# A twenty-first expert weight unit, and an output projection that gives its weights back unit by unit, in a two-layer decoder trunk

## The reference

```
for i in range(2):
    mod = cond @ ada_w[i] + ada_b[i]                 # six vectors of 1024
    h = modulate(rms_norm(x, norm_mix[i]), sh_m, sc_m)
    y = diff_attention(h, ...) if i == 0 else mla_attention(h, ...)   # each ends in "@ w_o"
    x = x + g_m * y
    h = modulate(rms_norm(x, norm_ffn[i]), sh_f, sc_f)
    x = x + g_f * hier_moe(h, ...)   # 4 groups x 8 experts, top-1 group, top-2 experts in it
```

## Time and profile before

| | |
|---|---|
| median of 3 runs | 1125.56 us (1124.77 to 1127.2) |
| the profiled execution: its own time | 1125.21 us |
| the profiled execution: span of the trace | 1123.4 us |
| busy in the span: PE / DVE / ACT / POOL | 93% / 54% / 29% / 8% |
| moved by DMA | 341.44 MB, mean 304 GB/s |
| share of the chain that ended last: PE / DMA / DVE | 72% / 10% / 8% |

### The profile page before, as it was taken

How to read it: one execution, slowest core, us unless ns; L and a number is a source line. 1 busy time by engine, 2 the same in 40 slices (tenths; PEclk the granted TensorE clock), 3 DMA queues, 4 the chain that set the end, 5 groups by cost and what they waited for, 6 DMA issues and landing times.

```text
span 1123.4 us, 15296 instructions
## 1 busy us (share of the span) xinstructions
PE 1041.6 (93%) x5662; PEld 633.0 (56%) x5662; DVE 610.0 (54%) x1467; ACT 326.9 (29%) x889; POOL 92.1 (8%) x129
## 2 busy tenths in 40 slices
PE   7999999999998999897889999999998899979986
PEld 5444444656467666564556566555457666646652
DVE  6899989898647322222246577877236622222224
ACT  4321112874231111111114555665122211111110
POOL 1000000000011112121000000000001112101100
PEclk8999999999998999999999999999998999999999
DMA  9929868928569999999996400502717899999998
GB/s 367 405 89 378 354 259 322 419 101 325 200 255 372 408 419 420 417 418 419 419 386 275 164 1 1 188 1 84 329 75 277 351 420 420 418 413 419 420 415 336
DMA packets 66814, 341.44 MB, mean 304 GB/s; under 512 B 11110, under 2 KB 11366, under 8 KB 36400
## 3 DMA queue, kind: packets, MB, share of 16 engines
q1 hardware_dynamic: 49952, 297.68, 65.5%
q0 software_dynamic: 15120, 37.63, 8.6%
q10 hardware_dynamic: 1664, 5.09, 1.2%
HBM read 320.90 MB, written 37.24 MB: 319 GB/s over the span
## 4 chain that ended last, share of the span: by engine, by line
PE 72%; DMA 10%; DVE 8%; ACT 4%; issue 3%; SPq 3%; DVEq 0%; ACTq 0%; POOLq 0%
PE PP L956 17%; PE PP L722 10%; PE PP L832 10%; PE PP L971 8%; DMA ring<-in_moe_w 3%; DMA ring<-in_ada_t 3%; PE PP L744 3%; PE PP L1173 3%; PE PP L1139 2%; PE PP L1177 2%; PE PP L929 2%; PE PP L792 2%; SPq L566 2%; DMA X<-kept_d 2%; PE PP L781 2%
## 5 line engine op out<-in xcount | busy, mean ns | idle before, releaser
L722 PE MATMUL PP<-ring,AHS 128*128 128x512 f32 x320 | 139.9, 592 | 0.0
L2096 DVE TENSOR_TENSOR PS<-PS,PP 128x256 f32<-128x256 f32 x33 | 13.9, 421 | 194.8 <-PE PP L956 185.2
L832 PE MATMUL PP<-ring,AHS 128*128 128x512 f32 x256 | 112.2, 594 | 0.0
L2103 DVE SCALAR_TENSOR_TENSOR PS<-PP,small,GF 128x512 f32<-128x512 f32 x66 | 46.5, 746 | 110.7 <-PE PP L971 100.2
L722 PEld LDWEIGHTS PP<-ring,AHS 128*128 128x128 f32 x320 | 59.7, 190 | 69.8 <-issue 69.6
L956 PE MATMUL PP<-RQK,RV 128*64 128x256 f32 x640 | 75.4, 393 | 10.0 <-issue 7.7
L832 PEld LDWEIGHTS PP<-ring,AHS 128*128 128x128 f32 x256 | 47.8, 190 | 56.9 <-issue 56.9
L956 PE MATMUL PP<-ring,RV 128*64 128x256 f32 (+1 forms) x608 | 73.8, 383 | 4.5 <-ACT RV L1590 1.7
L1614 ACT ACTIVATE PS<-PP 128x256 f32<-128x256 f32 x33 | 12.7, 384 | 214.7 <-PE PP L956 136.7
L956 PEld LDWEIGHTS PP<-RQK,RV 128*64 128x64 f32 x640 | 56.4, 142 | 31.8 <-issue 17.6
L956 PE MATMUL PP<-AHS,RV 128*64 128x256 f32 x640 | 71.9, 380 | 2.3 <-issue 2.2
(11 more groups left out here) (359 smaller groups left out, 1677.5 us busy)
## 6 DMA issues: line engine op xcount, KB each, us to landing
AHS<-in_moe_w SPq DMA_DIRECT2D x61, 1024.0 KB
ring<-in_moe_w SPq DMA_DIRECT2D x58, 1024.0 KB, 21.9
RQK<-in_moe_w SPq DMA_DIRECT2D x52, 1024.0 KB
ring<-in_ada_t SPq DMA_DIRECT2D x22, 1024.0 KB, 21.2
AHS<-in_ada_t SPq DMA_DIRECT2D x18, 1024.0 KB
X<-in_moe_w SPq DMA_DIRECT2D x16, 1024.0 KB, 24.7
ring<-in_da_w_qkv SPq DMA_DIRECT2D x10, 1024.0 KB, 13.2
RQK<-in_ada_t SPq DMA_DIRECT2D x8, 1024.0 KB
```

The source lines that it names most:

```text
L722: last = mm(PB[qkv_bank(n)][:, :], HT[:, c, t * P:(t + 1) * P], us[c // 4][:, (c % 4) * NH:(c % 4 + 1) * NH], start=c == 0, stop=c == C - 1)
L832: last = mm(PB[2 * t + n][:, :], (OT, OTM)[l][:, k, t * P:(t + 1) * P], us[k // 2][:, (k % 2) * D + n * NH:(k % 2) * D + (n + 1) * NH], st ...
L2103: last = stt(ysb[b][:, cols], PB[5 + m][:, :], weight, GF[:, cols], ALU.mult, ALU.mult)
```

## The change

- There are 21 slots: a tile `spare` of 8 KB a partition is the last one. The DMA descriptor area of a partition, `dynamic_dma_scratch_size`, is set to 8192 bytes.
- In layer 0 SP asks for the unit of this slot amid the projections, ahead of the 23rd entry of the first stream (SPARE_AT). In layer 1 it asks for it after the units of slots 12 and 13, when three tiles of the residual of layer 1 are done.
- The order of slots starts with AHS and RQK in both layers. The requests ahead of the routing keep their order by slots.
- The fourth tile's output product is done by weight units: units 0 and 1 for both halves, counting after each; then units 2 and 3, half by half. The counts at which w_o's units are free are 7, 8, 10 and 10 of ten (MIXED). VectorE waits for counts 9 and 10 for this tile.
- Waits for "a" ahead of the reload of X become waits for "y" of the same pair.

```diff
-SLOTS = BANKS * RING + 2
+SLOTS = BANKS * RING + 3
+SPARE_AT = 22
+MIXED = (2 * T - 1, 2 * T, 2 * T + 2, 2 * T + 2)
...
-    first += [(("wo", u), wo[:, 2 * u:2 * u + 2, :], 2, 2 + u, ("wo", 2 * T)) for u in range(4)]
+    first += [(("wo", u), wo[:, 2 * u:2 * u + 2, :], 2, 2 + u, ("wo", MIXED[u])) for u in range(4)]
...
+        spare = sb("spare", [P, UNIT])
...
-            slot_order.append(unheld + held[:2] + [16, 17, 12, 13, 14, 15] + list(range(RING, 2 * RING)) + held[2:] + [18, 19])
+            slot_order.append([16, 17, 12, 13, 14, 15] + list(range(RING, 2 * RING)) + unheld + held + [18, 19, SLOTS - 1])
...
+                    if l == 0 and n == SPARE_AT:
+                        first_units(0, SLOTS - 1)
                     if l == 1 and n == 0:
-                        sp.wait_ge(sem("a"), LAST - 1)
+                        sp.wait_ge(sem("y"), LAST - 1)
...
+                elif slot == SLOTS - 1:
+                    if l:
+                        sp.wait_ge(sem("res"), T + 3)
...
+            def first_units(l, *slots):
+
+                for slot in slots:
+                    expert_unit(l, slot_order[l].index(slot))
...
-                    for u in (0, 1, 10, 11, 12, 13):
-                        expert_unit(0, u)
+                    first_units(0, 0, 1, 6, 7, 8, 9)
...
-                    for u in (14, 15, 2, 3, 6, 7, 16, 17, 8, 9):
-                        expert_unit(0, u)
+                    first_units(0, 10, 11, 2, 3, 12, 13, 4, 5, 14, 15)
                 else:
-                    for u in (0, 1, 10, 11, 12, 13, 14, 15, 4, 5, 6, 7, 2, 3, 16, 17, 8, 9):
-                        expert_unit(1, u)
+                    first_units(1, 4, 5, 6, 7, 8, 9, 10, 11, 16, 17, 12, 13, SLOTS - 1, 0, 1, 2, 3, 14, 15)
...
-                experts(l, BANKS, (2, 3, 4, 5))
+                experts(l, BANKS, (3, 4, 5))
...
+                def last_product():
+
+                    t = T - 1
+                    for u in range(2):
+                        for n in range(2):
+                            last = mixed(l, t, n, us, (2 * u, 2 * u + 1))
+                        last.then_inc(sem("wo"), 1)
+                    for n in range(2):
+                        mixed(l, t, n, us, range(C // 2, C)).then_inc(sem("wo"), 1)
...
-                product(3)
+                last_product()
...
-                    m = 8 * l + 2 * t + n
-                    dve.wait_ge(sem("wo"), m + 1)
+                    dve.wait_ge(sem("wo"), MIXED[-1] * l + 2 * t + n + (3 if t == T - 1 else 1))
...
-    nc = bacc.Bacc("TRN2", target_bir_lowering=False, num_devices=1)
+    nc = bacc.Bacc("TRN2", target_bir_lowering=False, num_devices=1, dynamic_dma_scratch_size=8192)
```

More of the change, by code:

```diff
@@ L220, in ring_plan @@
     wo = A["mla_w_o"][0].rearrange("(k p) n -> p k n", p=P)
-    second += [(("wo", u), wo[:, 2 * u:2 * u + 2, :], 2, ("wo", 4 * T)) for u in range(4)]
+    second += [(("wo", u), wo[:, 2 * u:2 * u + 2, :], 2, ("wo", MIXED[-1] + MIXED[u])) for u in range(4)]
     second = [(key, src, k, n % RING, free) for n, (key, src, k, free) in enumerate(second)]
@@ L438, in unit @@
                 return ring[:, s, :]
+            if s == SLOTS - 1:
+                return spare[:, :]
             if s >= X_SLOT:
@@ L452, in build @@
         loaded = {}
-        fills[X_SLOT:] = [1, 1]
+        fills[X_SLOT:] = [1, 1, 1]
         for l in range(2):
@@ L474, in build @@
         for t in range(T):
-            own = in_x_slot if t < 2 else 0
+            own = in_x_slot if t < 3 else 0
             loaded["rows", t] = 16 * (1 + own + 2)
@@ L478, in build @@
             loaded["last rows", t] = loaded["mla", t] + 16 * (own + 1)
-        s_w = [sem(f"w{s}") for s in range(X_SLOT)] + [sem("xl0"), sem("xl1")]
+        s_w = [sem(f"w{s}") for s in range(X_SLOT)] + [sem("xl0"), sem("xl1"), sem("xl2")]
         w1 = [A["moe_w1"][l].rearrange("g e (p c) f -> (g e) p (c f)", c=C) for l in range(2)]
@@ L532, in free_at_first @@
                 elif slot < 2 * RING + 2:
-                    sp.wait_ge(*((sem("omla"), 8) if l else (sem("wo"), 2 * T)))
+                    sp.wait_ge(*((sem("omla"), 8) if l else (sem("wo"), MIXED[-1])))
                 elif slot < 2 * RING + 4:
@@ L580, in _ @@
                 if l == 0:
-                    for u in (0, 1, 10, 11, 12, 13):
-                        expert_unit(0, u)
+                    first_units(0, 0, 1, 6, 7, 8, 9)
                     for entry in late[0:2]:
                         load_unit(*entry)
-                    for u in (4, 5):
-                        expert_unit(0, u)
+                    first_units(0, 16, 17)
                     for entry in late[2:]:
                         load_unit(*entry)
-                    for u in (14, 15, 2, 3, 6, 7, 16, 17, 8, 9):
-                        expert_unit(0, u)
-                else:
-                    for u in (0, 1, 10, 11, 12, 13, 14, 15, 4, 5, 6, 7, 2, 3, 16, 17, 8, 9):
-                        expert_unit(1, u)
+                    first_units(0, 10, 11, 2, 3, 12, 13, 4, 5, 14, 15)
+                else:
+                    first_units(1, 4, 5, 6, 7, 8, 9, 10, 11, 16, 17, 12, 13, SLOTS - 1, 0, 1, 2, 3, 14, 15)
                 for b in range(2):
                     sp.wait_ge(sem(f"gath{b}"), 16 * (PAIRS // 2 * l + 1))
-                for u in (18, 19):
-                    expert_unit(l, u)
-                experts(l, BANKS, (2, 3, 4, 5))
+                first_units(l, 18, 19)
+                experts(l, BANKS, (3, 4, 5))
                 for n in range(BANKS + 1, BETWEEN):
@@ L623, in _ @@
                 last_experts(l)
-            sp.wait_ge(sem("a"), PAIRS + LAST - 1)
+            sp.wait_ge(sem("y"), PAIRS + LAST - 1)
             for t in range(T):
```

## The result

The changed kernel takes **1119.4 us** (median of 7, 1115.11 to 1121.59) beside 1124.77 for before in the same rounds: ratio 0.995, 95% interval 0.9936 to 0.9964, that is 5.6 us less (4.0 to 7.2). Two further measurements of it gave 0.9952 [0.9935, 0.997] and 0.9954 [0.9938, 0.9971]. The forecast was 1122.8 and its range ended at 1120.0: the sign was right, the size was half of what came, and the time lay just under the range, near the 1120.3 of rival A.

A forecast was written before the change was run, and what follows sets the result against it. Expert phases were taken as bound by saturated DMA, with TensorE starved for layer 0's last weights. Terms 0 - 2.53 - 0.2 + 0 + 0, with a tenth for layer 1's hole, gave -2.8: 1125.56 becomes 1122.8 us, range 1120.0 to 1125.0.

The forecast's parts named there:

- rival A: Layer 1's unit pays too, last transfers being late for the sum of bytes: another 2.5 us, 1120.3 us; chance 0.13.
- Part 1: Layer 0's twenty-first unit, loaded amid the projections: early load costs 0, one unit less returns -2.53 us, bounds -2.2 to -2.9.
- elsewhere there is room: Outside both layers' expert phases, DMA engines were said to be below their limit of 408 to 420 GB/s.
- Part 2: Output weights released unit by unit in the fourth tile's product: -0.2 us, bounds 0 and -1.0.
- the cover of keep_busy: Layer 0's routing: first gather lands 2.9 us earlier, but keep_busy ends at 352.36, so only 0.2 us reach TensorE.
- the other clock as a term of the range: TensorE's clock stretches may fall otherwise when everything moves by 3 us: 1.4 us to either side.
- the queue then dries until pair 0 frees slots: Layer 0, start of experts: X units leave before 352.95, but the emptied queue was taken to limit the return.
- Part 3: Layer 1's twenty-first unit: load costs nothing, returns 0 because SP pauses for the overflow tile; bounds -0.4, if wrong -2.53.
- the backlog ran dry just as SP resumed: Layer 1, end of SP's overflow pause: 352 and 360 GB/s, limit near 418, read as the request list running out.
- that distance unchanged within 0.5 us: Sign of being right: from layer 1's first expert product to the end, the time stays the same.
- Parts 4 and 5: New order of slots, and half the DMA descriptor area felt only by GpSimd's gathers and scatters: 0 each.
- The 358 GB/s: Skill's HBM-side bound set against the measured 410 to 415 GB/s; by it a unit would be worth 2.93 us.

The follow-up runs named there:

- x2_release: Kernel before with the early release alone (fourth output product by weight units, w_o units counted one by one), 20 slots: 0.9996 to before.
- v3_release: Same kernel as x2_release, measured a second time: 0.9985 to before.
- w1_l0late: Changed kernel, but layer 0's twenty-first unit asked for only when pair 0 has given slots back: 0.9941 to before.
- v1_l0late: Same kernel as w1_l0late, measured a second time beside the changed kernel: 0.996 to before.
- z_after: The changed kernel measured once more, without any edit: 0.9952 to before.
- v2_after: The changed kernel measured yet again, without any edit: 0.9954 to before, 1118.91 us.
- x4_l1late: Changed kernel, but layer 1's twenty-first unit asked for only when pair 0 has given slots back: 0.9969 to before.
- y1_short: Changed kernel with one unit (pair 10, k = 5) asked for behind SP's pause, not ahead of it: 0.9979 to before.
- y2_long: Changed kernel with four more units (pair 11) asked for ahead of SP's pause in layer 1: 0.9936 to before.
- x3_spare: Changed kernel without the early release, that is 21 slots with the fourth output product whole again: 0.9955 to before.
- y5_post: Kernel before, one layer 1 unit behind SP's pause (pair 12) loaded only to an eighth: 0.9963 to before.
- x1_area: Kernel before with only the DMA descriptor area halved to 8192 bytes: 0.9995 to before.
- y3_blong: Kernel before (20 slots) with the first four units of pair 11 asked for ahead of SP's pause: 1.0005 to before.
- y4_pre: Kernel before, one layer 1 unit ahead of SP's pause (pair 8) loaded only to an eighth: 0.9972 to before.

## Why the prediction was wrong in size

**Part 1, the unit of layer 0: right mechanism, a little too large.** Forecast -2.53. Distance 0 falls from 231.0 to 229.0 with the unit alone, and from 229.4 (x2_release, v3_release, w1_l0late, v1_l0late) to 227.3 (after, z_after, v2_after, x4_l1late, y1_short, y2_long) with the release: -2.0 and -2.1, under my lower bound of 2.2 (-1.4 to -2.5 in the rows of the table). What takes the rest isn't shown. I had bounded a hole behind the X units at some tenths, and with the unit alone it stayed so: over the 16 us behind the first freed slots x3_spare lacks 0.8 us of transfers against 412 GB/s, before 0.6. With the release the hole is larger. In z_after, where the X units were asked for early, the windows just behind the first freed slots (SP at 359.31) are not full, and it lacks 2.9 us:

```profile
354.00:356.00 2.00, 1.34 (x13) 1.08 (x13) 1.36 (x5) 1.46 (x4) 0.25 (x1) 1.00 0.80 336
356.00:358.00 2.00, 2.00 (x23) 1.57 (x20) 1.79 (x11) 1.33 (x2) 0.75 (x1) 1.00 1.00 422
358.00:360.00 2.00, 2.00 (x22) 1.61 (x20) 1.79 (x7) 0.39 (x1) 0.00 (x0) 1.00 0.80 318
360.00:362.00 2.00, 2.00 (x22) 1.61 (x20) 1.93 (x4) 0.00 (x0) 0.00 (x0) 1.00 0.80 262
```

The price of its early load was 0: the last keep_busy starts at 344.43 in before and at 344.56 in after. Over all profiles it starts at 344.3 to 344.6 in twelve and at 346.1 to 346.4 in six, with and without the early unit in both groups (y5_post and w1_l0late have 346.1 and 346.4 without it), and why isn't known. The forecast's "elsewhere there is room" passed over two slices of before, the second with 405 GB/s and the eighth with 419; the load, asked for at 79.44 us, falls into neither.

**Part 2, the early release: the first step that failed, the cover of keep_busy.** Forecast -0.2. Measured on the means -1.2 (distance 0 from 231.0 to 229.8) to -1.7 (from x3_spare's 229.0 to 227.3, the mean with both), and in the rows of the table -0.6 to -1.0 under the long keep_busy and -2.2 to -2.3 under the shorter ones; in the times 0.9996 and 0.9985. The gather's own time was right (4.3 forecast, 4.37 measured). Two things behind it were wrong. First, I took keep_busy's 7.93 us for its length. It was an execution with the low clock in it: with none, 5.18 us, keep_busy hides nothing and pair 0 starts 2.9 us sooner (x1_area and x2_release). Of the sixteen profiles with 44 records eight have 5.2 or 6.8 us. I had listed the other clock as a term of the range, of either sign and taken apart from the release, and not asked what the release is worth under it. Secondly, I dismissed the sooner X units with "the queue then dries until pair 0 frees slots". In a phase that ends when the sum of the bytes has come, what moves before that point can count, though the queue is dry behind it. With keep_busy at its long 7.9 us, SP asks for them 3.1 us ahead of pair 0 in z_after (352.51 and 355.60) where before had 1.4. At 3.7 us behind pair 0's start, when its first slots come free, SP's queue had moved 91.2 MB in z_after and in x4_l1late, but 90.5 in x3_spare, which has no release: 0.7 MB that the phase no longer has to carry, 1.7 us. The hole shown above takes most of it back: distance 0 is 228.78 and 228.09 in these two and 228.99 in x3_spare.

**Part 3, the unit of layer 1: the second step that failed, the price of 0 for it.** Forecast 0, with a tenth for the old hole; by the times x4_l1late, without it, loses 1.7 to 2.1 us. The mechanism was right, but not that it takes back the whole unit. The hole came. But "the backlog ran dry just as SP resumed" was read from 352 to 369 GB/s, and a rate of 0.85 of the limit is a queue that still has work. At the resumption SP's queue had 39.78 MB still to move in before and 38.98 in after, of which 38.8 MB belong to requests behind the pause (33 units, the reload of X and the output): before had 0.98 MB of its list outstanding, 2.4 us, and after 0.18. Such a backlog is what a unit more can use up at a profit before a hole opens. y3_blong agrees (nothing to be had in before), and so does y4_pre (a unit less ahead of the pause paid 2.4 us on distance 1). Over the profiles the mean hole grew from 0.33 us (before, x1_area, x2_release, v3_release, y5_post) to 2.23 (after, z_after, v2_after, w1_l0late, v1_l0late, x3_spare). Of the unit's 2.5 us that leaves 0.6, the mean of distance 1 gives 0.85 (246.83 to 245.98), and x4_l1late's ratio 1.7 to 2.1. These means mix early and late resumptions, and the late ones (134.4 us) are all on the side of twenty-one units. At the same kind of resumption distance 1 falls by 2.3 and 2.7 us from before and x1_area (247.98 and 247.46), but by 0.7 and 0.8 from the two profiles with the release alone (246.32 and 245.55). Why those two are shorter isn't known; the release touches w_o's counts in layer 1 as well, and I had priced nothing for that. The forecast's own sign, "that distance unchanged within 0.5 us", failed by -2.35 in the profiled execution, with a resumption of the same kind as in before (133.0 and 133.3 us). Rival A, with 2.5, had too much for the list of after: y2_long took another 1.8.

**Parts 4 and 5.** No run shows a cost of the slot order; none was made for it alone. The area's 0 stood, to within 1.0 us of cost. The Trainium skill (SBUF — State Buffer, SBUF size: 192, 224, or 256?) puts it at 16 KiB; half of that sufficed here, for requests of 128 rows.

**The unit's price.** The saturated slices of after stand at 416 to 420 GB/s, so a unit is 2.5 us, and the distances gave back 2.0 to 2.1. The 358 GB/s that the forecast set against the rows is the wrong figure here, and its 2.93 us would have been further off. The Trainium skill has the fitting one on another page (HBM Reference, Specifications (TRN2)): a core that streams alone gets about 425 GB/s, and 358 is each core's share when both of a pair stream. The trace agrees, with 416 to 420.

**The sum again**, from the profiles: -2.0 for the unit and -1.7 for the release in layer 0 (distance 0, 231.0 to 227.3), -0.6 to -0.9 for layer 1, together -4.3 to -4.6. The times say -5.2 to -5.6, each with 1.6 to 2.0 us of uncertainty. My sum of 2.8 was short by the release (1.0 to 1.5 us on these means), then by layer 1 (0.5 to 0.8 by the profiles, 1.7 to 2.1 by x4_l1late's time), and over by half a microsecond for layer 0's unit. One measure takes in everything from the start of the last keep_busy of layer 0 to the end of SP's last operation: 776.8 and 777.5 us in before and x1_area, 775.2 and 775.3 with the release alone, 774.1 with the unit alone, and 771.0, 772.3 and 772.4 in the three profiles of after. So the whole change takes 5.3 us off it, as the times say. **Open:** without one layer's unit it is 772.3 (x4_l1late), 771.3 and 773.2 (w1_l0late, v1_l0late), hardly more than after, and by the times w1_l0late lacks nothing of the gain. So the split between release, layer 0's unit and layer 1's isn't settled; it rests on parts of profiles, on x3_spare and on x4_l1late, and not on every run.

## What to carry to other kernels

Ask of a cover how long it is at both clocks before you say that it hides something: 44 keep_busy matmuls covered most of a 2.9 us gain in one execution and none of it in the next, and 28 of them did not hold pair 0 in two profiles. In a phase bound by bytes a request that leaves sooner can pay even if the queue is dry for a while behind it; here 1.7 us of transfers moved ahead left 0.2 to 0.9 us in layer 0. Where the engine that asks must pause, size the list ahead of the pause with the ring, and judge whether it ran dry by the bytes outstanding at the resumption, not by a dip in GB/s.

## What the runs showed of the hardware

The lower clock granted to TensorE (1.2 GHz) falls on the overflow product for nothing, for some 3 us or for some 7 us, from one execution to the next: in z_after, after and v2_after, the same kernel, the resumption came at 131.7, 133.0 and 134.5 us. In layer 0 it falls on the first keep_busy, on the last one, or on both, and the same 44 matmuls take 5.2, 6.8 or 7.9 us. Through the pause of one queue the hole varies by up to 2.6 us with it. That is half of what was to be measured. The times of one kernel spread over 2.4 to 9.1 us here; how much of that is this clock wasn't separated.
